# Scan stage of a gated linear recurrence: the sums of squares of seven heads as two f32r products instead of one fp32 product

## The chip, the cores and the metric

One NeuronCore of a Trainium2 chip runs the whole program, a chain of two small transformer blocks in float32 at batch 1 and 256 positions. The metric is the device time of one execution in microseconds; before the change its median is 1361.3 us over three runs (1361.16 to 1363.24).

Engines by their names in the profile: PE is TensorE (PEld its weight loads), DVE VectorE, ACT ScalarE, POOL GpSimd, SP SyncE, which issues the weight DMAs. Each engine runs its instructions in program order; they meet through semaphores alone.

## What is computed

The program runs `first_block` and `second_block`, each of two layers with a mixer and a convolutional feed-forward part. The change lies in the HGRN2 mixer of the second block: a gated linear recurrence, forward and backward, of eight heads, followed by an RMS norm of each head's output over its 128 channels.

```python
def rmsnorm(x, g):
    xf = x.astype(F32)
    y = xf * lax.rsqrt(jnp.mean(xf * xf, axis=-1, keepdims=True) + NORM_EPS)
    return (y * g.astype(F32)).astype(x.dtype)

def mixer_hgrn2(u, mem_kv, w_in, lb_fwd, lb_bwd, norm_g, w_out):
    ...
    o = (gla_chunked(q, k_f, v, lf_f)
         + flip_t(gla_chunked(flip_t(q), flip_t(k_b), flip_t(v), flip_t(lf_b))))
    o = rmsnorm(o, norm_g.reshape(HG_HEADS, HG_VAL_DIM)).reshape(bsz, t, HG_W).astype(u.dtype)
    o = o * jax.nn.silu(gate)
    return jnp.concatenate([o, memory_cross_attn(xq, mem_kv)], axis=-1) @ w_out
```

The mean of squares in `rmsnorm` is what the change touches.

## The kernel before

Every weight matrix is streamed from HBM in tiles of 128 x 2048 floats into three buffers `raw`. ACT copies a tile into `whi` with rounding to f32r (L296), and DVE (L319), POOL (L304) or both subtract this from the original to give the low part `wlo`. Activations are kept in the same way as a high and a low part, in `XS` (input of a mixer) and `MS` (its output, 12 chunks; `ms_high` on ACT, L528, and `ms_low` on DVE, L532). A projection is then the high weights times both parts of the activations (L388, L389), and the low weights times the high part (L395); the output projection is L460 and L471 in the same manner.

The scan stage works on 128 channels of one head on the partitions and 256 positions on the free axis. It is a software pipeline written out by hand, with a loop over n in `hgrn_pe`, `hgrn_act` and `hgrn_dve`; the order of the calls in these loops is each engine's order. In step n, PE projects z of head n, forms the values of head n-2 (`values_pe`, L2306, into the PSUM bank HVAL), projects q and the gate of head n, sums the squares of head n-2 (`squares_pe`, L2315), and forms the scores of head n-1 (`scores_pe`, L2282 to L2295). "Head h" below means the step in which its squares are summed, n = h + 2; from n = 8 on PE works on the output projection in place of z and q.

ACT in step n: logarithms of the gates (L2349, after a table load L2343), a weight copy L296, the exponentials (L2358 to L2360), the root of head n-3 (`root_act`, L2398 and L2400: logarithm, then exponential), a table load and two sigmoids of z (L2369, L2370), a weight copy, the squares of head n-2 (L2379: it reads HVAL and writes SR in SBUF), `ms_high` of head n-3, and the sigmoid of q and gate (L2387).

DVE in step n: gates (L2484, L2485), masks on the scores of head n-2 (L2516, L2517) with four small additions (L2523), the running sums and their differences of head n-1 (L2493 to L2509), a low weight part of 2048 columns (L319), the factors of head n-1 (L2535 to L2549, the last of them L2546), the normed output of head n-3 (L2468), then `UG`, value times gain times gate of head n-2 (L2472), then `ms_low` of head n-3 (L532), and a low part of 1024 columns (L319).

Two orders matter. DVE's L2472 waits for the squares L2379 of the same head (`h_sr`), since two engines don't read a PSUM bank at a time here. ACT's L2358 waits for DVE's differences (`h_di`). POOL takes the other 1024 columns of a low part; in steps 1 and 2 it starts once L2546 is done, in steps 3 to 7 once `ms_low` L532 is done, after the loop once the last L2546 is done.

The sum over partitions is a product with a matrix of ones: `C("ones")` as weights, the squares as moving data, the result on all 128 partitions of HSUM. Both are float32, and PE runs a float32 product as more than one pass.

Of the kernel before, what the change touches and what calls it, by code (L numbers as in the profile page):

```python
# [7 lines left out]
F32 = mybir.dt.float32  # L8
# [3 lines left out]
ALU = mybir.AluOpType  # L12
ACT = mybir.ActivationFunctionType
# [160 lines left out]
def program(nc, T, out):  # L174
    with ExitStack() as ctx:
        pe, ve, ac, po, sp = nc.tensor, nc.vector, nc.scalar, nc.gpsimd, nc.sync

        def sem(name):
            return ctx.enter_context(nc.semaphore("s_" + name))

        def mark(name):
            return Mark(sem(name))

        def sb(name, shape, dt=F32):
            return ctx.enter_context(nc.sbuf_tensor(name, shape, dt))
# [5 lines left out]
        MS = sb("MS", [128, 12, 512], F32R)  # L191
# [22 lines left out]
        def C(name, rows=128):  # L214
            a, b = CC[name]
            return cc[0:rows, a:b]

        def col(name, i=0, rows=128):
            a = PC[name][0] + i
            return pc[0:rows, a:a + 1]  # L220
# [124 lines left out]
        def act_weights(m):  # L345
            while ahead["act"] <= min(m, NTILE - 1):
                high_part(ahead["act"])
                ahead["act"] += 1
# [672 lines left out]
        def soft_act(h, base, s, P, NM, segs, sink=None):  # L1021
            nm, p = NM[h % 4], P[h % len(P)]
            ac.wait_ge(a_mx.sem, base + h + 1)
            if h >= len(P):
                ac.wait_ge(a_tn.sem, base + h - len(P) + 1)
            for i, (a, b) in enumerate(segs):
                ins = ac.activation(p[:, a:b], s[h % 2][:, a:b], ACT.Exp, bias=nm[:, i:i + 1], accum_out=nm[:, 2 + i:3 + i])
            if sink is not None:
                ins = ac.activation(nm[:, 6:8], nm[:, 0:2], ACT.Exp, bias=sink[0])
            ins.then_inc(a_ex.up())  # L1030
# [825 lines left out]
        def cross_query_act(X, j):  # L1856
            ac.wait_ge(w_done, DONE[X.m0 + j])
            ac.activation(X.XQ[:, 512 * j:512 * j + 512], X.pbank[j][:, :], ACT.Copy,
                          scale=float(np.float32(128 ** -0.5))).then_inc(X.xq.up())
# [313 lines left out]
        SR, RS = R(256), R(256)  # L2173
# [11 lines left out]
        MAIN, DIAG, HVAL, HSUM = bank[4], bank[5], bank[6], bank[7]  # L2185
# [6 lines left out]
        h_vn, h_sz, h_sq, h_gt, h_lf = (mark("h_" + k) for k in ("vn", "sz", "sq", "gt", "lf"))  # L2192
        h_di, h_de, h_fa, h_sc, h_mk = (mark("h_" + k) for k in ("di", "de", "fa", "sc", "mk"))

        h_va, h_sr, h_su, h_rs, h_ug, h_on = (mark("h_" + k) for k in ("va", "sr", "su", "rs", "ug", "on"))
        lo0 = PC["lbl"][0]
        l0, l1 = pc[:, lo0:lo0 + 16], pc[:, lo0 + 16:lo0 + 32]
# [2 lines left out]
        def at_z(h):  # L2200
            return ht + 2 * h

        def at_q(h):
            return ht + 2 * h + 1
# [104 lines left out]

        def squares_pe(h):  # L2310

            pe.wait_ge(h_sr.sem, h + 1)
            if h:
                pe.wait_ge(h_rs.sem, h)
            pe.matmul(HSUM[:, 0:256], C("ones")[:, 0:128], SR, start=True, stop=True).then_inc(h_su.up())  # L2315

        def hgrn_act():
            act_weights(hx + 1)
            ac.wait_ge(l_e.sem, 2)
            ac.activation(lb[:, 16:48], lb[:, 16:48], ACT.Exp).then_inc(l_x.up())  # L2320
            act_weights(hw)
            cross_query_act(X1, 0)
            act_weights(hw + 1)
            cross_query_act(X1, 1)
            act_weights(hw + 2)
            soft_act(0, HB, xS, hP, hNM, csegs)
            soft_act(1, HB, xS, hP, hNM, csegs)
            act_weights(at_z(0))
            copy_act(0, HB, xT, hPT, 512)
            soft_act(2, HB, xS, hP, hNM, csegs)  # L2330
            soft_act(3, HB, xS, hP, hNM, csegs)
            act_weights(at_q(0))
            for tt in range(2):
                for h in range(2):
                    ac.wait_ge(w_done, DONE[hw + 2] - 1 + tt)
                    ac.activation(HV[:, tt, 512 * h:512 * h + 512], accs[tt][h][:, :], ACT.Copy).then_inc(h_vn.up())
            act_weights(at_z(1))
            cross_split_act(0)
            cross_split_act(1)
            for n in range(11):  # L2340
                if 0 <= n - 1 < 8:
                    h = n - 1
                    nc.scalar.preload_act_table_set("natural_log_exp_and_others")  # L2343
                    ac.wait_ge(h_sz.sem, h + 1)
                    if h:
                        ac.wait_ge(h_di.sem, h)
                    for d in range(2):
                        o = 8 * d + h
                        ins = ac.activation(lf[:, d, 1:257], SZ[:, 256 * d:256 * d + 256], ACT.Ln, bias=lm[:, o:o + 1],  # L2349
                                            scale=e0[:, o:o + 1])  # L2350
                    ins.then_inc(h_lf.up())
                if n:
                    act_weights(min(at_z(n + 1), LAST[6]))
                if 0 <= n - 1 < 8:
                    ac.wait_ge(h_di.sem, h + 1)
                    if h:
                        ac.wait_ge(h_fa.sem, h)
                    ac.activation(PP, DD, ACT.Exp).then_inc(h_de.up())  # L2358
                    ac.activation(NN, DD, ACT.Exp, scale=-1.0).then_inc(h_de.up())
                    ac.activation(EG, AA, ACT.Exp).then_inc(h_de.up())  # L2360
                if 0 <= n - 3 < 8:
                    root_act(n - 3)
                if n < 8:
                    ac.wait_ge(w_done, DONE[at_z(n)])
                    if n >= 2:
                        ac.wait_ge(h_fa.sem, n - 1)
                    if n:
                        ac.wait_ge(h_lf.sem, n)
                    ac.activation(SZ, BZ[n % 2][:, :], ACT.Sigmoid)  # L2369
                    ac.activation(SN[n % 2], BZ[n % 2][:, :], ACT.Sigmoid, scale=-1.0).then_inc(h_sz.up())  # L2370
                if n == 0:
                    copy_act(2, HB, xT, hPT, 512)
                act_weights(min(at_q(n + 1), LAST[6]))
                if 0 <= n - 2 < 8:
                    h = n - 2
                    ac.wait_ge(h_va.sem, h + 1)
                    if h:
                        ac.wait_ge(h_su.sem, h)
                    ac.activation(SR, HVAL[:, 0:256], ACT.Square).then_inc(h_sr.up())  # L2379
                if 0 <= n - 3 < 8:  # L2380
                    ac.wait_ge(h_on.sem, n - 2)
                    ms_high(n - 3, ON[(n - 3) % 2])
                if n < 8:
                    ac.wait_ge(w_done, DONE[at_q(n)])
                    if n:
                        ac.wait_ge(h_gt.sem, n)
                    ac.activation(SQ, BQ[n % 2][:, :], ACT.Sigmoid).then_inc(h_sq.up())  # L2387
                if n == 0:
                    cross_split_act(2)
                    cross_split_act(3)  # L2390
            act_weights(NEXT[6])
# [14 lines left out]
        def cross_split_dve(i):  # L2406
            ms_low(8 + i, xT[i % 2][:, 0:256])

        def hgrn_dve():
# [41 lines left out]
            dve_weights(at_q(1))  # L2451
            cross_split_dve(2)
            cross_split_dve(3)
            for n in range(1, 11):
                if n - 1 < 8:
                    gates_dve(n - 1)
                if 0 <= n - 2 < 8:
                    masked_dve(n - 2)
                if n - 1 < 8:
                    differences_dve(n - 1)  # L2460
                dve_weights(min(at_z(n + 1), LAST[6]))
                if n - 1 < 8:
                    factors_dve(n - 1)
                if 0 <= n - 3 < 8:
                    h = n - 3
                    ve.wait_ge(h_rs.sem, h + 1)
                    ve.wait_ge(h_ug.sem, h + 1)
                    ve.tensor_tensor(ON[h % 2], UG[h % 2], RS, ALU.mult).then_inc(h_on.up())  # L2468
                if 0 <= n - 2 < 8:
                    h = n - 2  # L2470
                    ve.wait_ge(h_sr.sem, h + 1)
                    ve.scalar_tensor_tensor(UG[h % 2], HVAL[:, 0:256], col("bng", h), GT[h % 2], ALU.mult,  # L2472
                                            ALU.mult).then_inc(h_ug.up())
                if 0 <= n - 3 < 8:
                    ve.wait_ge(h_on.sem, n - 2)
                    ms_low(n - 3, ON[(n - 3) % 2])
                dve_weights(min(at_q(n + 1), LAST[6]))
# [354 lines left out]
```

## Time and profile before

| | |
|---|---|
| median of three runs | 1361.3 us |
| span of the profiled execution | 1361.3 us |
| PE busy | 1337.7 us, 98% |
| DVE busy | 1023.2 us, 75% |
| ACT busy | 783.7 us, 58% |
| POOL busy | 147.7 us, 11% |
| granted clock of PE, mean | 0.998 |
| scan stage | about 1028 to 1167 us |

The page gives busy time of each engine over the whole span. "Waits" give, for a stretch, who waited for whom. A timeline row reads: start and length in us, engine, line and operation, output and inputs by their tiles' names (`ar` is the arena that holds SR, UG and most of the stage's data, `ps` a PSUM bank, `cc` the constants), shapes, how many instructions are merged (xN), and in brackets how long the engine stood idle before it and what ended that. Instructions of one engine overlap a little: the next may start before the one ahead has ended.

### The profile page before, as it was taken

What the parts mean: (1) busy time and instruction counts of PE and PEld (TensorE: products, weight loads), DVE (VectorE), ACT (ScalarE), POOL (GpSimd) and SP (SyncE); (2) the same over time, 40 slices, a digit from 0 to 9 for tenths busy, and PEclk for the clock granted to TensorE, in tenths of its full rate; (3) what the DMA queues carried; (4) which work ended last, traced back from release to release, by engine and by line L of the source; (5) the groups of instructions that cost most, each with busy time, mean ns of one, the idle gap of its engine ahead of it and who ended that gap; (6) DMA issues with size and microseconds to landing.
All of it is one profiled execution on the core that took longest, in us unless ns stands there. A gap on an engine that the chain in (4) does not pass through costs nothing. (4 is left out here: it accounts for less than half of the span.)

```text
span 1361.3 us, 20748 instructions
## 1 busy us (share of the span) xinstructions
PE 1337.7 (98%) x8197; PEld 1160.3 (85%) x8197; DVE 1023.2 (75%) x1681; ACT 783.7 (58%) x1268; POOL 147.7 (11%) x131
## 2 busy tenths in 40 slices
PE   7999999999999999999999999999999999999998
PEld 7887888888898788887987888888789998888887
DVE  5866578777896788778788677666567997786765
ACT  5644266666443566554677566555557875655553
POOL 4770300000100000000000000000302224000000
PEclk9999999999999999999999999999999999999999
DMA  8623165655563455553543255555344345455551
GB/s 315 230 80 125 62 222 213 238 196 198 191 237 138 169 202 218 194 196 136 205 156 112 96 214 216 216 188 189 150 159 182 129 152 186 150 190 204 192 196 73
DMA packets 38175, 242.17 MB, mean 178 GB/s; under 512 B 4416, under 2 KB 6848, under 8 KB 10688
## 3 DMA queue, kind: packets, MB, share of 16 engines
q1 hardware_dynamic: 38080, 240.86, 48.5%
q8 instruction: 65, 1.06, 0.3%
q14 instruction: 30, 0.25, 0.1%
HBM read 236.89 MB, written 2.64 MB: 176 GB/s over the span
## 5 line engine op out<-in xcount | busy, mean ns | idle before, releaser
L319 DVE TENSOR_TENSOR wlo<-raw,whi 128x2048 fp32r<-128x2048 f32 (+1 forms) x179 | 401.2, 2246 | 102.4 <-ACT whi L296 100.4
L296 ACT ACTIVATE whi<-raw 128x2048 fp32r<-128x2048 f32 x195 | 370.5, 1904 | 83.7 <-PE ps L471 39.8
L408 PE MATMUL ps<-XS,whi 128*128 128x512 f32 x1392 | 331.7, 390 | 0.0
L408 PEld LDWEIGHTS ps<-XS,whi 128*128 128x128 f32 x1392 | 257.8, 188 | 52.1 <-issue 0.6
L460 PE MATMUL ps<-whi,MS 128*128 128x512 f32 x960 | 233.5, 391 | 0.0
L460 PEld LDWEIGHTS ps<-whi,MS 128*128 128x128 f32 x960 | 177.5, 188 | 35.9 <-issue 0.4
L413 PEld LDWEIGHTS ps<-XS,wlo 128*128 128x128 f32 x1392 | 178.5, 191 | 6.8
L413 PE MATMUL ps<-XS,wlo 128*128 128x256 f32 x1392 | 180.6, 283 | 0.0
L388 PE MATMUL ps<-XS,whi 128*128 128x256 f32 x672 | 168.0, 290 | 0.0
L389 PE MATMUL ps<-XS,whi 128*128 128x256 f32 x672 | 164.4, 284 | 0.0
L304 POOL TENSOR_TENSOR wlo<-raw,whi 128x512 fp32r<-128x512 f32 x90 | 124.2, 1410 | 195.0 <-ACT whi L296 107.0
L1540 ACT ACTIVATE ar<-ps 128x256 f32<-128x256 f32 x176 | 57.3, 377 | 146.1 <-PE ps L413 145.9
L388 PEld LDWEIGHTS ps<-XS,whi 128*128 128x128 f32 x672 | 129.6, 193 | 1.1 <-issue 0.3
L389 PEld LDWEIGHTS ps<-XS,whi 128*128 128x128 f32 x672 | 129.7, 193 | 0.4
L547 POOL TENSOR_TENSOR st<-st 128x1 f32<-128x1 f32 x24 | 16.7, 696 | 984.9 <-DVE st L724 521.5
L471 PE MATMUL ps<-wlo,MS 128*128 128x512 f32 x480 | 122.5, 389 | 0.0
L471 PEld LDWEIGHTS ps<-wlo,MS 128*128 128x128 f32 x480 | 90.1, 188 | 18.8
L1566 DVE TENSOR_TENSOR ar<-ps,ar 128x256 f32<-128x256 f32 x176 | 66.1, 418 | 43.4 <-ACT ar L1540 43.4
L395 PE MATMUL ps<-XS,wlo 128*128 128x256 f32 x672 | 88.4, 283 | 0.0
L395 PEld LDWEIGHTS ps<-XS,wlo 128*128 128x128 f32 x672 | 84.1, 192 | 0.0
L1546 ACT ACTIVATE ar<-ar,pc 128x256 f32<-128x256 f32 x88 | 40.1, 502 | 46.9 <-DVE ar L1566 46.9
L528 ACT ACTIVATE MS<-ar 128x256 fp32r<-128x256 f32 x104 | 42.2, 405 | 22.6 <-DVE ar L1595 9.6
(330 smaller groups left out, 1546.3 us busy)
## 6 DMA issues: line engine op xcount, KB each, us to landing
raw<-in_up SPq DMA_DIRECT2D x88, 1024.0 KB, 4.8
raw<-in_down SPq DMA_DIRECT2D x44, 1024.0 KB, 4.9
raw<-in_hg_t SPq DMA_DIRECT2D x16, 1024.0 KB, 4.8
raw<-in_od_t SPq DMA_DIRECT2D x8, 1024.0 KB, 5.6
raw<-in_ev_a SPq DMA_DIRECT2D x6, 1024.0 KB, 9.2
raw<-in_wa_o SPq DMA_DIRECT2D x6, 1024.0 KB, 4.9
raw<-in_hg_o SPq DMA_DIRECT2D x6, 1024.0 KB, 4.9
raw<-in_ev_o SPq DMA_DIRECT2D x4, 1024.0 KB, 5.9
```

The costliest lines, as they stand in the source:

```text
L296: ac.activation(parts_of(m)[0][:, 0:w], raw[m % NRAW][:, 0:w], ACT.Copy).then_inc(w_hi)
L304: ins = po.tensor_tensor(lo[:, c], r[:, c], hi[:, c].bitcast(F32), ALU.subtract)
L319: ve.tensor_tensor(lo[:, c], r[:, c], hi[:, c].bitcast(F32), ALU.subtract).then_inc(w_lo_v)
L388: pe.matmul(d, hi[:, c], XS[:, k, 0:256], start=(k == 0 and i == some[0]), stop=False)
L389: pe.matmul(d, hi[:, c], XS[:, k, 256:512], start=False, stop=False)
L395: last = pe.matmul(d, lo[:, c], XS[:, k, 0:256], start=False, stop=(k == 7 and i == some[-1]))
L408: pe.matmul(banks[i][:, 0:512], hi[:, c], XS[:, k, 0:512], start=(k == 0), stop=False)
L413: last = pe.matmul(banks[i][:, 0:256], lo[:, c], XS[:, k, 0:256], start=False, stop=(k == 7))
L460: pe.matmul(accs[tt][h][:, 0:c], x, hi[:, n * j + c * h:n * j + c * h + c], start=(begin and x is sh), stop=False)
L471: ins = pe.matmul(accs[tt][h][:, 0:c], sh, lo[:, n * j + c * h:n * j + c * h + c], start=False, stop=end)
L1540: ac.activation(o[:, 256 * i:256 * i + 256], b[:, 256:512], ACT.Copy).then_inc(f_cb.up())
L1566: ins = ve.tensor_tensor(o[:, c], up_banks(k, j)[i][:, 0:256], o[:, c], ALU.add)
```

## The change

For heads 0 to 6 ACT computes the square twice from HVAL: once rounded to f32r into `SRh` (a part of MS chunk 7, not yet in use), then as before in float32 into `SR`. DVE subtracts, SRl = SR - SRh, right behind L2472. PE multiplies a matrix of ones in f32r (`ONE`, in MS chunk 6, copied once ahead of the loop) with SRh as soon as that is there, and then with SRl, and adds both in HSUM. Head 7 keeps the float32 product, since MS chunk 7 and 6 are needed by then for the mixer's output. New semaphores are `h_sh` (SRh written) and `h_sl` (ONE and SRl written).

```diff
--- before.py
+++ after.py
@@ -2192,6 +2192,8 @@
         h_vn, h_sz, h_sq, h_gt, h_lf = (mark("h_" + k) for k in ("vn", "sz", "sq", "gt", "lf"))
         h_di, h_de, h_fa, h_sc, h_mk = (mark("h_" + k) for k in ("di", "de", "fa", "sc", "mk"))
 
+        h_sh, h_sl = mark("h_sh"), mark("h_sl")
+        ONE, SRh, SRl = MS[:, 6, 0:128], MS[:, 7, 0:256], MS[:, 7, 256:512]
         h_va, h_sr, h_su, h_rs, h_ug, h_on = (mark("h_" + k) for k in ("va", "sr", "su", "rs", "ug", "on"))
         lo0 = PC["lbl"][0]
         l0, l1 = pc[:, lo0:lo0 + 16], pc[:, lo0 + 16:lo0 + 32]
@@ -2309,10 +2311,17 @@
 
         def squares_pe(h):
 
-            pe.wait_ge(h_sr.sem, h + 1)
+            if h == 7:
+                pe.wait_ge(h_sr.sem, h + 1)
+                pe.wait_ge(h_rs.sem, h)
+                pe.matmul(HSUM[:, 0:256], C("ones")[:, 0:128], SR, start=True, stop=True).then_inc(h_su.up())
+                return
+            pe.wait_ge(h_sh.sem, h + 1)
             if h:
                 pe.wait_ge(h_rs.sem, h)
-            pe.matmul(HSUM[:, 0:256], C("ones")[:, 0:128], SR, start=True, stop=True).then_inc(h_su.up())
+            pe.matmul(HSUM[:, 0:256], ONE, SRh, start=True, stop=False)
+            pe.wait_ge(h_sl.sem, h + 2)
+            pe.matmul(HSUM[:, 0:256], ONE, SRl, start=False, stop=True).then_inc(h_su.up())
 
         def hgrn_act():
             act_weights(hx + 1)
@@ -2376,6 +2385,10 @@
                     ac.wait_ge(h_va.sem, h + 1)
                     if h:
                         ac.wait_ge(h_su.sem, h)
+                    if h < 7:
+                        ac.activation(SRh, HVAL[:, 0:256], ACT.Square).then_inc(h_sh.up())
+                    if h:
+                        ac.wait_ge(h_sl.sem, h + 1)
                     ac.activation(SR, HVAL[:, 0:256], ACT.Square).then_inc(h_sr.up())
                 if 0 <= n - 3 < 8:
                     ac.wait_ge(h_on.sem, n - 2)
@@ -2451,6 +2464,7 @@
             dve_weights(at_q(1))
             cross_split_dve(2)
             cross_split_dve(3)
+            ve.tensor_copy(ONE, C("ones")[:, 0:128]).then_inc(h_sl.up())
             for n in range(1, 11):
                 if n - 1 < 8:
                     gates_dve(n - 1)
@@ -2471,6 +2485,9 @@
                     ve.wait_ge(h_sr.sem, h + 1)
                     ve.scalar_tensor_tensor(UG[h % 2], HVAL[:, 0:256], col("bng", h), GT[h % 2], ALU.mult,
                                             ALU.mult).then_inc(h_ug.up())
+                    if h < 7:
+                        ve.wait_ge(h_sh.sem, h + 1)
+                        ve.tensor_tensor(SRl, SR, SRh.bitcast(F32), ALU.subtract).then_inc(h_sl.up())
                 if 0 <= n - 3 < 8:
                     ve.wait_ge(h_on.sem, n - 2)
                     ms_low(n - 3, ON[(n - 3) % 2])
```

## Rows read from the trace of the kernel before

**Rows 1.** Page, busy time of each engine, its share and instructions.
```profile
PE 1337.7 (98%) x8197; PEld 1160.3 (85%) x8197; DVE 1023.2 (75%) x1681; ACT 783.7 (58%) x1268; POOL 147.7 (11%) x131
```

**Rows 2.** Waits, 1040 to 1175 us: who waited for whom, total, times, longest.
```profile
ACT gb L2358 <- DVE ar L2509: 19.5, 7, 4.3
...
DVE ar L2472 <- ACT ar L2379: 5.3, 7, 1.2
...
DVE ar L2516 <- PE ps L2295: 1.7, 4, 0.8
...
PEld ps L2282 <- DVE ar L2546: 0.6, 1, 0.6
...
PEld ps L2315 <- ACT ar L2379: 0.2, 1, 0.2
```

**Rows 3.** Timeline of PE: start, us, instruction (heads 0, 1 and 4).
```profile
1055.17 0.60 PE L2315 MATMUL ps<-ar,cc 128*128 128x256 f32 x2
...
1069.60 0.60 PE L2315 MATMUL ps<-ar,cc 128*128 128x256 f32 x2
...
1070.13 0.28 PE L2282 MATMUL ps<-ar 128*32 128x32 f32 x7
...
1112.95 0.70 PE L2315 MATMUL ps<-ar,cc 128*128 128x256 f32 x2
...
1113.58 0.23 PE L2282 MATMUL ps<-ar 128*32 128x32 f32 x2
```

**Rows 4.** Timeline of PE, two f32r products of a projection.
```profile
1078.76 0.28 PE L388 MATMUL ps<-XS,whi 128*128 128x256 f32 x1
...
1078.88 0.28 PE L389 MATMUL ps<-XS,whi 128*128 128x256 f32 x1
```

**Rows 5.** Timeline of ACT, heads 1 to 5.
```profile
1068.37 0.39 ACT L2379 ACTIVATE ar<-ps 128x256 f32<-128x256 f32 x1
...
1068.63 0.43 ACT L528 ACTIVATE MS<-ar 128x256 fp32r<-128x256 f32 x1
...
1112.51 0.38 ACT L2379 ACTIVATE ar<-ps 128x256 f32<-128x256 f32 x1
...
1127.24 0.38 ACT L2379 ACTIVATE ar<-ps 128x256 f32<-128x256 f32 x1
```

**Rows 6.** Timeline of DVE, head 1.
```profile
1068.79 0.48 DVE L2472 SCALAR_TENSOR_TENSOR ar<-ps,pc,ar 128x256 f32<-128x256 f32 x1 [0.76 <-ACT ar L2379]
...
1069.19 0.41 DVE L532 TENSOR_TENSOR MS<-ar,MS 128x256 fp32r<-128x256 f32 x1
...
1069.52 1.22 DVE L319 TENSOR_TENSOR wlo<-raw,whi 128x1024 fp32r<-128x1024 f32 x1
```

**Rows 7.** Timelines of DVE and POOL, head 0.
```profile
1054.35 0.49 DVE L2472 SCALAR_TENSOR_TENSOR ar<-ps,pc,ar 128x256 f32<-128x256 f32 x1 [0.29 <-ACT ar L2379]
...
1054.75 1.81 DVE L319 TENSOR_TENSOR wlo<-raw,whi 128x1024 fp32r<-128x1024 f32 x1
...
1057.43 0.69 DVE L2516 TENSOR_TENSOR ar<-ps,cc 128x512 f32<-128x512 f32 x1 [0.21 <-PE ps L2295]
...
1054.18 3.52 POOL L304 TENSOR_TENSOR wlo<-raw,whi 128x512 fp32r<-128x512 f32 x2 [9.39 <-DVE ar L2546]
```

**Rows 8.** Timelines of DVE, POOL and PE, head 6.
```profile
1140.97 1.43 DVE L2546 TENSOR_TENSOR ar<-ar 128x256 f32<-128x256 f32 x4
...
1142.65 0.48 DVE L2472 SCALAR_TENSOR_TENSOR ar<-ps,pc,ar 128x256 f32<-128x256 f32 x1
...
1143.29 0.87 DVE L532 TENSOR_TENSOR MS<-ar,MS 128x256 fp32r<-128x256 f32 x1 [0.16 <-ACT MS L528]
...
1142.48 5.33 POOL L304 TENSOR_TENSOR wlo<-raw,whi 128x512 fp32r<-128x512 f32 x4 [8.88 <-DVE ar L2546]
...
1142.45 0.22 PE L2282 MATMUL ps<-ar 128*32 128x32 f32 x1 [0.24 <-DVE ar L2546]
```

**Rows 9.** Timeline of DVE ahead of the loop's first differences.
```profile
1032.70 0.62 DVE L2493 TENSOR_REDUCE ar<-ar 128x14 f32<-128x448 f32 x1 [1.33 <-ACT ar L2349]
```

**Rows 10.** Busy time by window: PE, PEld, DVE, ACT, POOL, granted clock, DMA.
```profile
1170.00:1180.00 10.00, 9.03 (x74) 8.55 (x74) 7.64 (x11) 6.62 (x10) 0.55 (x1) 1.00 0.01 2
```

## The prediction

> **What bounds the kernel now.** I read the page's busy line first: PE is busy in 98% of the span [rows 1], so at first sight every TensorE nanosecond saved is a nanosecond of the result. The waits of the scan stage (1040 to 1175 us) say something more particular [rows 2]. PE hardly waits there: 0.2 us once for the square L2379, 0.6 us once for DVE's factors L2546. But ACT and DVE wait for each other in every step: L2358 waits for DVE's L2509 seven times, 19.5 us in total, and L2472 waits for the square L2379 seven times, 5.3 us. Two engines that wait for each other once a step form a loop, and a loop has a period of its own.
>
> Its period stands in the start times. The squares of head 1 start at 1068.37 us on ACT, those of head 5 at 1127.24: 58.87 us for four heads, 14.72 a head [rows 5]. PE's product of the squares starts at 1055.17 for head 0 and at 1069.60 for head 1: 14.43 a head; by head 4 it starts at 1112.95, (1112.95 - 1069.60) / 3 = 14.45 [rows 3]. So PE is 0.3 us a head faster than the loop and eats a margin. At head 1 the square is there (1068.37 + 0.39 = 1068.76) 0.84 us before PE takes it up at 1069.60. At head 4 the margin is gone: that is the 0.2 us wait. **From head 4 on the DVE and ACT loop sets the pace**, not PE.
>
> The loop, once round: L2472 on DVE, the low part L532, weight splits, gates, masks, differences to L2509; ACT then takes the exponentials from L2358 (which waits 2.8 us a head for L2509, 19.5 / 7), the root, a table load, two sigmoids, a whole weight copy, and the squares L2379; L2472 waits for these. In a step I find no other gap in it that matters.
>
> **The change part by part.** (1) PE. The full fp32 product is two records, 0.60 us together with a mean near 0.38, so the second starts 0.22 us after the first; the first score product starts at 1070.13, 0.53 after 1069.60 [rows 3]. Consecutive f32r products of the same 256 columns start 0.12 apart [rows 4]. Two of them, plus the 0.09 left over before the scores (0.53 less two times 0.22), are 0.33: **0.20 us a head, 1.4 us for seven heads**, where nothing makes PE wait.
>
> (2) ACT gets one more square ahead of the old one. L528 starts 0.26 after L2379 [rows 5], so the old square, and DVE's L2472 behind it, come 0.26 later. L528, the gate sigmoid L2387 and the next table load are queued behind and come as much later, less than what (3) adds on DVE before their results are read. The old square's new wait, for SRl of the head before, ended a round earlier. Lower end nothing, were ACT waiting there anyway (it isn't: L2379 has no idle before it); upper end the whole 0.39 of the square. I take 0.26, the start-to-start time of the nearest pair.
>
> (3) DVE gets the subtraction SRl between L2472 and L532. It has the shape and operands of L532, whose successor L319 starts 0.33 later (1069.19 to 1069.52); L2472's successor starts 0.40 after it [rows 6]. So everything from L532 on comes 0.33 later, GpSimd's split too, which waits for L532. Both pieces lie in the loop: its period goes **from 14.72 to about 15.31**, +0.59 a head.
>
> (4) PE's second product now waits for SRl, and scores and the next z projection are queued behind it. After L2472 starts, SRl ends 0.40 + 0.41 later. A product that was blocked shows the rest of the path: at head 4 the square ended at 1112.51 + 0.38 = 1112.89 [rows 5], the scores started at 1113.58 [rows 3], 0.69 with two slots of 0.22; with one f32r slot of 0.11 it is 0.36. Scores start 1.17 after L2472 starts. For head 1 that is 1068.79 + 0.26 + 1.17 = 1070.22 even with no earlier delay, against 1070.13 now. The saving of (1) is thus behind a wait in every head, and I count it at nothing.
>
> (5) Head 0 is special: GpSimd's split of two operations runs from 1054.18, 3.52 us, and DVE's L319 of 1024 columns, issued at 1054.75, takes 1.81 [rows 7] where it takes 1.22 alone [rows 6]. One of the two engines stands while the other works on SBUF. With L319's 1.1 us inside, a GpSimd operation is (3.52 - 1.1) / 2 = 1.2 to 1.25 us, the first until about 1055.45. After the change L2472 starts at 1054.35 + 0.26, SRl is issued at 1055.01, into that operation; it ends about 1055.78. If GpSimd's second operation then goes ahead of L319 (to 1057.03), L319 ends at 1058.15 instead of 1056.56: 1.59 late, less the 0.3 that the masks L2516 stand now (0.21 idle, and 0.08 of overlap as between L532 and L319): **+1.3**. If L319 goes first it is +0.4 (the scores' end then counts). By the Trainium skill (SBUF — State Buffer, "SBUF: two separate sides") the engine that starts first holds the shared port pair for its whole instruction and the other blocks; the rows agree. GpSimd's second operation is by then the longer waiting, so I take 1.3.
>
> (6) Head 6: scores of head 7 start now when L2546 is done (1140.97 + 1.43 = 1142.40; PE at 1142.45) [rows 8]. DVE runs L2472 only after that, at 1142.65, and now PE must wait for SRl behind it. SRl would be issued at 1143.05, inside GpSimd's operation begun at 1142.48; L532, issued at 1143.29, shows what happens: 0.87 instead of 0.41, end at 1144.15. SRl ends at about that time, scores follow 0.36 later, 1144.51 instead of 1142.45: **+2.05**. Lower end, no contention: SRl ends at 1143.46, +1.37.
>
> (7) The copy of ONE comes before the loop, where DVE is idle 1.33 us before L2493 [rows 9]; some 0.2 us, nothing; were that gap missing it would cost its 0.2 once. No DMA, and nothing on SP's queue, is added or moved. Head 7 is unchanged.
>
> **The sum.** Start of L2472 of head 1: +1.3 (head 0) +0.26. Four more rounds to head 5: 4 x 0.59 = 2.36, so +3.9. There L532 and what follows it come 0.33 later, and so do the factors L2546 of the next step: +4.25. Head 6: +2.05. **PE reaches the scores of head 7 6.3 us late.** From there to the end of the span PE runs one product after another in an order that nothing here shortens, and its waits in the norms are for work that hangs on PE itself; all 6.3 us stay. The profiled execution's span is 1361.3 us, equal to the median of the runs: 1361.3 + 6.3 = **1367.6 us**. With the low ends of (5) and (6): 6.3 - 0.9 - 0.7 = 4.7, 1366.0. With the second square at 0.39 instead of 0.26 in six rounds (+0.8) and the masks' small operations one GpSimd turn later (+0.2): 1368.6.
>
> **The rivals.**
> Rival A, the loop is longer by one of the two pieces only. Some waits that I don't see inside the loop (for GpSimd's split, which stretches the small additions after the masks) could swallow 0.26 or 0.33 a round. For it: DVE also waits 1.7 us in four steps for L2295 of the scores [rows 2], so the loop has soft places. Against: the rounds of heads 1 to 5 average 14.72 though L2516 waits in a part of them only. Five rounds less 0.26 to 0.33 are 1.3 to 1.6 off, 4.7 to 5.0 late; with the low ends of (5) and (6) too, 3.1 to 3.4: 1364.2 to 1366.0, about 1365.3.
> Rival B, the other side: PE stays the bound. If ACT and DVE made up their own lengthening, the second product would find SRl ready and each of seven heads would save 0.20: 1361.3 - 1.4 = 1359.9, that is no measurable change. It decides at the square's end against PE: SRl needs 0.26 + 0.04 + 0.40 + 0.41 + 0.05 = 1.16 us after the old square's end to be ready, less the 0.12 by which the second product comes later. The largest margin in the trace, 0.86 at head 0 (its square ends 0.04 before L2472 starts, at 1054.31; PE is there at 1055.17), is under these 1.04, so it would need a shorter loop than the rows show.
> Rival C, more than the sum: DVE and GpSimd exclude each other at more places than (5) and (6), each turn costing up to 1.25 us: 1368.6 to 1372.
> Rival D, the clock: PE would now stand about 1.1 us in each step. In 1170 to 1180 it stands 0.97 of 10 us and the granted clock is 1.00 [rows 10], the level of 2.4 GHz. By the Trainium skill (Perfetto Trace Analysis, "Matmul Optimizations") the engine scales with utilization, so products should be issued back to back. If the steps of heads 1 to 5, some 75 us, ran at 1.2 GHz the time would be far over 1400 us; the row with as large a share of idle time speaks against it.
> Rival E, that f32r products of this form cost as much as the fp32 one: (1) would be nothing, and the sum hardly moves (+0.1 in head 6), since PE waits for SRl anyway. It is inside the forecast's own range.
>
> **How the numbers follow.** Forecast 0.68 (1366.0 to 1368.6, with E inside), A 0.14, B 0.06, C 0.10, D 0.02. The range takes in the forecast with its bounds, most of A and the nearer part of C: 1364.8 to 1369.8. About 0.2% (2.7 us) is what a measurement of this kernel tells from no change: slower by more means over 1364.0. All of forecast, C, D and nearly all of A: 0.91; within 0.2%: B and a little of A, 0.08; faster by more, 0.01, since (1) gives 0.1% at most.
>
> **What would show it.** In the profile after: L2379's two squares 0.26 apart; starts of L2472 15.3 us apart from head 1 on; PE waiting for DVE's SRl at every head, about 1.1 us a round from head 2 to 5 and about 2 us at head 6; L319 of head 0 stretched well over 1.8 us; L2509 of head 5's step 4.2 us late; nothing given back after the scores of head 7. I am wrong if the starts of L2472 stay 14.7 apart (the loop isn't closed as I say), if PE's waits at the squares are absent (B), or if the lateness at head 7's scores shrinks before the end.

## The result and the profile after

The changed kernel took 1369.88 us in the median of six runs (1368.14 to 1371.92), the kernel before, beside it and earlier, 1361.23 (1360.52 to 1363.24, six runs). The ratio is 1.0062 with a 95% interval of 1.0052 to 1.0072: slower by 8.65 us. On a second chip it was 1370.48 against 1361.75, ratio 1.0065 (1.0052 to 1.0077). Forecast were 1367.6 us and slower; the median lies 2.3 us above the forecast and 0.1 us above the end of the range, 1369.8. Taken by the ratio, 1.0062 times the 1361.3 from which the forecast set out is 1369.7, just inside. The range was met at its very edge, and with nothing to spare.

The profiled execution after has a span of 1366.8 us. Its own time was 1368.14: in every run whose span is on record the time is 1.2 to 1.4 us more than the span, 1.3 in most.

Spans of single executions carry differences that arise long before the stage, so the two profiles are compared from a common mark inside it: the first score product of head 0, before which the change does nothing on PE, to the first score product of head 7, behind which it does nothing either. Timelines of PE, before and then after:

```profile
1041.27 0.28 PE L2282 MATMUL ps<-ar 128*32 128x32 f32 x7
```

```profile
1038.78 0.28 PE L2284 MATMUL ps<-ar 128*32 128x32 f32 x7
```

Before, head 7's scores start at 1142.45 [rows 8]: 101.18 us. After, they start at 1146.38: 107.60. **The stage is 6.42 us longer; the sum said 6.3.** The page in short, after: PE busy 1338.3 us (98%), DVE 1024.0, ACT 784.5, POOL 147.4; the work is hardly more, the order of waits is what changed. The waits of 1040 to 1180 us, against [rows 2] (L2367, L2526, L2486, L2392 are the L2358, L2509, L2472, L2379 of before; L2324 is PE's second product, L2490 DVE's subtraction):

```profile
ACT gb L2367 <- DVE ar L2526: 24.2, 7, 4.8
...
DVE ar L2486 <- ACT ar L2392: 10.0, 7, 4.3
...
PEld ps L2324 <- DVE MS L2490: 7.9, 7, 2.6
```

PE, which hardly waited, now waits for the subtraction in all seven heads, 7.9 us. DVE waits 10.0 us for the square where it waited 5.3. Of these 4.7 us more, the extra square ahead of the one it needs makes 0.27 in each of the heads 0 to 5, 1.6 in all. The other 3.1 are one wait in head 7 (4.25 us, before 1.16), which lies behind head 7's scores and costs nothing, since the time from there to the end is the same as before where the clock doesn't fall (the column "rest" below). Timeline of PE in heads 1 and 6, against [rows 3, 8]; L2322 is the first product, L2324 the second, L2284 the scores:

```profile
1067.53 0.28 PE L2322 MATMUL ps<-MS 128*128 128x256 f32 x1
...
1068.54 0.39 PE L2324 MATMUL ps<-MS 128*128 128x256 f32 x1 [0.74 <-DVE MS L2490]
...
1068.86 0.28 PE L2284 MATMUL ps<-ar 128*32 128x32 f32 x7
...
1146.07 0.39 PE L2324 MATMUL ps<-MS 128*128 128x256 f32 x1 [2.30 <-DVE MS L2490]
...
1146.38 0.28 PE L2284 MATMUL ps<-ar 128*32 128x32 f32 x7
```

The first product starts 1.01 us before the second, ahead of which PE stands idle for the subtraction; the scores follow 0.32 later. At head 6 the stand is 2.30 us long. Timelines of DVE in heads 0, 4 and 5, of ACT in head 4 and of POOL in head 0, against [rows 5 to 7]:

```profile
1052.12 0.48 DVE L2486 SCALAR_TENSOR_TENSOR ar<-ps,pc,ar 128x256 f32<-128x256 f32 x1 [0.56 <-ACT ar L2392]
...
1052.52 0.74 DVE L2490 TENSOR_TENSOR MS<-ar,MS 128x256 fp32r<-128x256 f32 x1
...
1053.18 2.30 DVE L319 TENSOR_TENSOR wlo<-raw,whi 128x1024 fp32r<-128x1024 f32 x1
...
1113.65 0.48 DVE L2486 SCALAR_TENSOR_TENSOR ar<-ps,pc,ar 128x256 f32<-128x256 f32 x1 [1.04 <-ACT ar L2392]
...
1114.05 0.42 DVE L2490 TENSOR_TENSOR MS<-ar,MS 128x256 fp32r<-128x256 f32 x1
...
1114.38 0.42 DVE L532 TENSOR_TENSOR MS<-ar,MS 128x256 fp32r<-128x256 f32 x1
...
1128.97 0.48 DVE L2486 SCALAR_TENSOR_TENSOR ar<-ps,pc,ar 128x256 f32<-128x256 f32 x1 [1.04 <-ACT ar L2392]
...
1112.96 0.38 ACT L2389 ACTIVATE MS<-ps 128x256 fp32r<-128x256 f32 x1
...
1113.22 0.40 ACT L2392 ACTIVATE ar<-ps 128x256 f32<-128x256 f32 x1
...
1051.68 2.71 POOL L304 TENSOR_TENSOR wlo<-raw,whi 128x512 fp32r<-128x512 f32 x2 [9.38 <-DVE ar L2563]
```

In head 4 everything is as in the sum: squares 0.26 apart, L2486 to L2490 0.40, then 0.33, and 15.32 us from one L2486 to the next (1113.65 to 1128.97) where it was 14.72. In head 0 the subtraction L2490 takes 0.74 and L319 of 1024 columns 2.30 instead of 1.81, while GpSimd's two operations take 2.71 together instead of 3.52: they end at 1054.39, and L319 1.09 later, at 1055.48. GpSimd's second operation thus went ahead of L319. Timelines of DVE and POOL in head 6, against [rows 8]:

```profile
1142.85 1.42 DVE L2563 TENSOR_TENSOR ar<-ar 128x256 f32<-128x256 f32 x4
...
1144.92 1.09 DVE L2490 TENSOR_TENSOR MS<-ar,MS 128x256 fp32r<-128x256 f32 x1
...
1145.93 1.50 DVE L532 TENSOR_TENSOR MS<-ar,MS 128x256 fp32r<-128x256 f32 x1
...
1144.35 5.46 POOL L304 TENSOR_TENSOR wlo<-raw,whi 128x512 fp32r<-128x512 f32 x4 [9.11 <-DVE ar L2563]
```

The factors L2563 end at 1144.27; the subtraction, issued at 1144.92, 0.57 after GpSimd began, takes 1.09 instead of 0.41 and ends at 1146.01, and PE starts 0.06 later.

One step is longer than the sum has it: from L2472 of head 5 to the factors. In that step no weight split stands ahead of DVE's masks, and DVE waits there for PE's scores; in the changed kernel these are themselves behind the subtraction. The masks, before and then after:

```profile
1130.04 0.69 DVE L2516 TENSOR_TENSOR ar<-ps,cc 128x512 f32<-128x512 f32 x1 [0.84 <-PE ps L2295]
```

```profile
1131.90 0.69 DVE L2533 TENSOR_TENSOR ar<-ps,cc 128x512 f32<-128x512 f32 x1 [1.11 <-PE ps L2297]
```

They start 2.38 us after L2472 before (at 1127.66), 2.93 after (1128.97): 0.55 later, where the sum has 0.33.

What the sum doesn't hold at all is PE's clock. Busy time by window (PE, PEld, DVE, ACT, POOL, then the granted clock) around the stand at head 6:

```profile
1140.00:1147.00 7.00, 4.70 (x69) 3.63 (x67) 6.90 (x14) 5.55 (x9) 2.65 (x2) 1.00 0.70 263
...
1147.00:1152.00 5.00, 5.00 (x29) 4.13 (x24) 4.06 (x8) 0.63 (x2) 2.81 (x3) 0.66 0.33 93
```

PE was busy 4.70 of 7 us, then the granted clock is 0.66 on average over the next 5 us: part of it at 1.2 GHz in place of 2.4. From head 7's scores to the end of the span it is 220.46 us here and 218.86 before. The kernel before has such a fall as well, but far from the stage, at its start:

```profile
40.00:45.00 5.00, 5.00 (x30) 4.67 (x28) 3.68 (x12) 4.43 (x6) 1.05 (x1) 0.66 1.08 391
```

### The profile page after: what moved, and what is told of

It reads as the page before. It is cut to its first block and busy times, and to the rows that moved or that the text cites. A ratio compares the mean times of both kernels' runs of the same rounds, so it can differ in the third digit from the quotient of the medians.

```text
span 1366.8 us, 20763 instructions
## 1 busy us (share of the span) xinstructions
PE 1338.3 (98%) x8197; PEld 1160.9 (85%) x8197; DVE 1024.0 (75%) x1689; ACT 784.5 (57%) x1275; POOL 147.4 (11%) x131
## 5 line engine op out<-in xcount | busy, mean ns | idle before, releaser
L319 DVE TENSOR_TENSOR wlo<-raw,whi 128x2048 fp32r<-128x2048 f32 (+1 forms) x179 | 401.5, 2248 | 102.2 <-ACT whi L296 100.2
L528 ACT ACTIVATE MS<-ar 128x256 fp32r<-128x256 f32 x104 | 42.1, 405 | 22.3 <-DVE ar L1595 9.6
## 6 DMA issues: line engine op xcount, KB each, us to landing
raw<-in_up SPq DMA_DIRECT2D x88, 1024.0 KB, 4.8
raw<-in_down SPq DMA_DIRECT2D x44, 1024.0 KB, 4.9
raw<-in_hg_t SPq DMA_DIRECT2D x16, 1024.0 KB, 4.8
raw<-in_od_t SPq DMA_DIRECT2D x8, 1024.0 KB, 5.7
raw<-in_ev_a SPq DMA_DIRECT2D x6, 1024.0 KB, 8.9
raw<-in_wa_o SPq DMA_DIRECT2D x6, 1024.0 KB, 4.9
raw<-in_hg_o SPq DMA_DIRECT2D x6, 1024.0 KB, 4.8
raw<-in_ev_o SPq DMA_DIRECT2D x4, 1024.0 KB, 5.9
```

The costliest lines, as they stand in the source:

```text
L319: ve.tensor_tensor(lo[:, c], r[:, c], hi[:, c].bitcast(F32), ALU.subtract).then_inc(w_lo_v)
```

## The experiments

The yardstick in the table is the one above, first scores of head 0 to first scores of head 7 in the profile, less the 101.18 us of before. "Rest" is from there to the end of the span. The last column is the median less that of the kernel before on the same chip, with the interval of the ratio.

| kernel | stage, us | rest, us | median less before, us (ratio, 95%) |
|---|---|---|---|
| before | 0 | 218.86 | |
| changed | +6.42 | 220.46 | +8.65 (1.0052 to 1.0072) |
| changed, again | +6.43 | 220.38 | +8.73 (1.0052 to 1.0077) |
| second square alone | +1.38 | 218.85 | +1.89 (1.0006 to 1.0024) |
| subtraction alone | +2.86 | 218.85 | +2.92 (1.0010 to 1.0027) |
| PE's products alone | -0.18 | 218.85 | -0.12 (0.9987 to 1.0005) |
| changed, head 6 in fp32 | +4.42 | 220.39 | +5.12 (1.0020 to 1.0045) |
| changed, head 0 in fp32 | +5.38 | 220.38 | +6.40 (1.0033 to 1.0060) |
| before, squares early | -0.09 | 220.88 | +0.23 (0.9994 to 1.0012) |
| changed, squares early | +3.23 | 220.73 | +4.85 (1.0024 to 1.0049) |
| both: squares early, head 6 in fp32 | +1.20 | 219.34 | +1.44 (1.0004 to 1.0023) |
| changed, stands filled | +6.46 | 218.87 | +6.28 (1.0033 to 1.0058) |
| before, one stand | +2.37 | 220.48 | +4.93 (1.0019 to 1.0041) |
| before, one stand filled | +2.33 | 218.86 | +3.06 (1.0013 to 1.0031) |

### The three parts, each alone

The second square alone:

```diff
+                    if h < 7:
+                        ac.activation(SRh, HVAL[:, 0:256], ACT.Square).then_inc(h_sh.up())
                     ac.activation(SR, HVAL[:, 0:256], ACT.Square).then_inc(h_sr.up())
```

> The kernel before, with the extra ACT square into SRh alone (nothing reads it; PE keeps its fp32 product, DVE has no subtraction). Loop theory: the period of the DVE and ACT loop grows by 0.26 us to 14.98, six times to the factors that the scores of head 7 wait for: 1.3 to 1.5 us later, 1361.2 + 1.3 = 1362.5 us. PE-bound rival: the square is hidden, 1361.2. Where the clock of PE falls to its lower level now and then because PE stands, about as often as in the kernel before.

The stage came out 1.38 us longer. L2472 (here L2476) on DVE, heads 1 and 5:

```profile
1068.62 0.49 DVE L2476 SCALAR_TENSOR_TENSOR ar<-ps,pc,ar 128x256 f32<-128x256 f32 x1 [1.04 <-ACT ar L2383]
...
1128.60 0.48 DVE L2476 SCALAR_TENSOR_TENSOR ar<-ps,pc,ar 128x256 f32<-128x256 f32 x1 [1.04 <-ACT ar L2383]
```

59.98 us for four rounds, 15.00 each; before, 14.72. The loop takes up 0.28 a round, no less than the start-to-start time of the square, 0.26.

The subtraction alone:

```diff
+                    if h:
+                        ac.wait_ge(h_sl.sem, h)
                     ac.activation(SR, HVAL[:, 0:256], ACT.Square).then_inc(h_sr.up())
 ...
+                    if h < 7:
+                        ve.tensor_tensor(SRl, SR, M32, ALU.subtract).then_inc(h_sl.up())
```

> The kernel before, with DVE's extra subtraction alone (SR minus a tile of constants, 256 columns, SBUF to SBUF, behind L2472; nothing on PE waits for it). Loop theory: +0.33 a round, and in head 0 it meets GpSimd's operation: if GpSimd's second operation then goes ahead of the weight split, +1.3 there, 2.9 us in all, 1364.1 us; if the split goes first, +2.0, 1363.2. PE-bound rival: 1361.2.

It was 2.86 us in the stage and 2.92 in the medians. Heads 1 and 5:

```profile
1069.30 0.48 DVE L2476 SCALAR_TENSOR_TENSOR ar<-ps,pc,ar 128x256 f32<-128x256 f32 x1 [0.76 <-ACT ar L2383]
...
1129.58 0.48 DVE L2476 SCALAR_TENSOR_TENSOR ar<-ps,pc,ar 128x256 f32<-128x256 f32 x1 [0.77 <-ACT ar L2383]
```

15.07 a round, +0.35, and nothing on PE waits for this subtraction: it costs by delaying DVE alone. From the first scores of head 0 to head 1's L2476 it is 28.63 us where it was 27.52: the subtraction of head 0 costs 1.1.

PE's products alone (SRl is a tile of zeros here, so the low part of the squares is left out):

```diff
+            pe.matmul(HSUM[:, 0:256], ONE, SRh, start=True, stop=False)
+            pe.matmul(HSUM[:, 0:256], ONE, SRl, start=False, stop=True).then_inc(h_su.up())
 ...
+                    ac.activation(SRh if h < 7 else SR, HVAL[:, 0:256], ACT.Square).then_inc(h_sr.up())
```

> The kernel before with PE's part alone: heads 0 to 6 as two f32r products, of the f32r square and of a tile of zeros, with no second square and no subtraction, so the low part of the squares is left out. Loop theory: PE saves 0.20 us a head, but from head 4 on it waits for the loop, so only head 0's 0.2 us reaches the end: 1361.0. PE-bound rival: 7 x 0.20 = 1.4 us, 1359.8.

First scores of heads 1, 2 and 7 on PE:

```profile
1055.22 0.28 PE L2284 MATMUL ps<-ar 128*32 128x32 f32 x7
...
1069.44 0.28 PE L2284 MATMUL ps<-ar 128*32 128x32 f32 x7
...
1141.99 0.28 PE L2284 MATMUL ps<-ar 128*32 128x32 f32 x7 [0.61 <-DVE ar L2556]
```

1055.22 to 1069.44 is 14.22 where the round was 14.43: the saving of 0.20 us a head is real while PE leads. But head 7 waits, as before, for the factors (L2546, here L2556), and the stage gains 0.18 in all. Even free of cost on DVE and ACT, PE's part is worth 0.2 us, and the medians can't tell it from nothing.

### The two special heads

Head 6 of the changed kernel in fp32, without second square and subtraction:

```diff
-            if h == 7:
+            if h >= 6:
 ...
-                    if h < 7:
+                    if h < 6:
```

> The changed kernel with head 6 as head 7: fp32 product of SR, no second square, no subtraction, so PE doesn't wait there for DVE's subtraction. Loop theory: the wait of head 6 goes (2.05 us of the sum of 6.3), and the 1.6 us of a fallen clock with it if the long stand of PE at head 6 is what lets it fall: 1361.2 + 4.3 = 1365.5 us. If the clock falls because of the 1.1 us stands in every step instead, the loss above the sum stays: 1361.2 + 8.6 - 2.05 = 1367.8 us.

```profile
1039.53 0.28 PE L2284 MATMUL ps<-ar 128*32 128x32 f32 x7
...
1145.13 0.28 PE L2284 MATMUL ps<-ar 128*32 128x32 f32 x7 [0.25 <-DVE ar L2563]
```

105.60 us between these two, +4.42: **2.00 us** less than the change, where 2.05 were expected. The median is +5.12, between the two expectations for the clock, and the profile has a fall again, this time in the norm behind the stage. So the mechanism of head 6 is shown; what the falls of the clock do is left open by this run.

Head 0 likewise:

```diff
-            if h == 7:
+            if h in (0, 7):
 ...
-                    if h < 7:
+                    if 0 < h < 7:
```

> The changed kernel with head 0 too in fp32 as before (no second square, no subtraction there), heads 1 to 6 as in the change. If DVE's subtraction of head 0 costs more than its own length because it meets GpSimd's operation (GpSimd's second operation goes ahead of the weight split, as the first profile of the change suggests: 1.36 us at the next L2472, 1.1 more than the second square's 0.26), the scores of head 7 start 6.4 - 1.1 = 5.3 us later than before, and the median is that of the changed kernel less 1.1. If head 0 costs no more than any other head (0.59), it is 5.8, 0.6 less.

The stage is +5.38, 1.04 less than the change: head 0 costs 1.04 us where another head costs about 0.6. The next L2472 follows 14.71 us later:

```profile
1053.90 0.48 DVE L2487 SCALAR_TENSOR_TENSOR ar<-ps,pc,ar 128x256 f32<-128x256 f32 x1 [0.29 <-ACT ar L2393]
...
1068.61 0.48 DVE L2487 SCALAR_TENSOR_TENSOR ar<-ps,pc,ar 128x256 f32<-128x256 f32 x1 [1.04 <-ACT ar L2393]
```

15.55 in the changed kernel (1067.67 less 1052.12), and there head 0's own L2486 comes 0.26 later after the first scores of head 0 (13.34 us against 13.08). That makes 1.10 us for head 0, where (5) of the prediction had 1.3.

### Is the loop closed through the squares?

The squares moved ahead of ACT's weight copy, first in the kernel before:

```diff
-                act_weights(min(at_q(n + 1), LAST[6]))
                 if 0 <= n - 2 < 8:
                     ...
+                act_weights(min(at_q(n + 1), LAST[6]))
                 if 0 <= n - 3 < 8:
                     ac.wait_ge(h_on.sem, n - 2)
```

> The kernel before with one move on ACT: the squares L2379 ahead of the weight copy that stood before them, 1.9 us earlier. Loop theory: DVE no longer waits 0.76 us for them, the loop could go round in 13.96 us, under PE's 14.43, so PE sets the pace to head 5: the waits of heads 4 and 5 go (0.05 and 0.3 us) and that of head 6 shrinks, 0.5 to 0.7 us less in all, 1361.5 - 0.6 = 1360.9. Rival (DVE doesn't get ahead, as GpSimd's split and the masks hold it): 1361.5.

My expectation fell: nothing was gained. Timelines of ACT and DVE:

```profile
1109.53 0.39 ACT L2378 ACTIVATE ar<-ps 128x256 f32<-128x256 f32 x1
...
1109.79 1.93 ACT L296 ACTIVATE whi<-raw 128x2048 fp32r<-128x2048 f32 x1
...
1111.60 0.42 ACT L528 ACTIVATE MS<-ar 128x256 fp32r<-128x256 f32 x1
...
1110.90 0.48 DVE L2472 SCALAR_TENSOR_TENSOR ar<-ps,pc,ar 128x256 f32<-128x256 f32 x1
...
1112.12 0.43 DVE L532 TENSOR_TENSOR MS<-ar,MS 128x256 fp32r<-128x256 f32 x1 [0.74 <-ACT MS L528]
```

DVE's L2472 no longer waits for the square, but the next instruction, L532, now waits 0.74 us for ACT's L528, which stands behind the same copy. The loop closes one instruction later and its round is 14.70, as good as the 14.72 of before. PE itself is no longer held at heads 4 and 5 (its scores of head 6 come 0.45 us earlier), but head 7's wait for the factors takes that back. The same with head 6 in fp32 on top of the change:

> The changed kernel with two moves: both squares ahead of the weight copy on ACT, and head 6 in fp32 as head 7. Loop theory: period 15.33 - 1.04 = 14.3, about PE's own 14.2, no wait for DVE's subtraction at head 6; the scores of head 7 wait for the factors L2546 as in the kernel before with the same move: 0.6 us less than the kernel before, 1360.9, where the changed kernel is 6.4 us later. If the order on ACT were not what closes the loop, the time would be that of the change without head 6: 1361.5 + 4.4 = 1365.9.

Also short of what I expected (+1.20 in place of -0.6), for the same reason. Its round is 14.98, and DVE waits for L528 even behind the subtraction:

```profile
1112.88 0.43 DVE L532 TENSOR_TENSOR MS<-ar,MS 128x256 fp32r<-128x256 f32 x1 [0.69 <-ACT MS L528]
```

So the subtraction costs nothing here, as DVE would only have waited longer, and the 0.28 that the round has above 14.70 is the second square alone. It is still 3.2 us less than head 6 in fp32 alone, so the order on ACT carries about half of what the change costs. And the change with the move, head 6 as changed:

> The changed kernel with the squares ahead of ACT's weight copy and head 6 still with its subtraction. With the order alone the loop went round in 14.98 us (with six heads) instead of 15.33, since DVE's L532 then waits for L528 behind the copy. So the scores of head 7 come 1.2 us late as with six heads, plus the wait for the subtraction at head 6, 2.0 us: 3.2 us, against 6.4 for the change, 1361.6 + 3.2 = 1364.8, and up to 1.6 more if the stand at head 6 lets the clock fall. If moving the squares had been worth nothing by itself: 1369.5.

+3.23 in the stage, as expected from the two parts (1.2 and 2.0), and +4.85 in the median; its profile has a fall right at the stand of head 6 (granted clock 0.66 from 1143 to 1148 us). No version with both new pieces beats the kernel before; the best, +1.44 us, is still slower, as its interval lies wholly above 1. The early squares also lengthen the rest by 0.3 to 0.5 us, where L603 of the norm waits 1.5 us for DVE instead of 1.0; I didn't follow that.

### The clock

The changed kernel once more:

> The changed kernel once more, on the same chip as the next three. Loop theory: its scores of head 7 start 6.4 us later after the stage's start than before, as in the first profile; what is above that in the time is falls of PE's clock, about 1.6 us each in the profile. If a fall belongs to the long stand of PE at head 6, its profile has one behind head 6 again, and its median is 1361.5 + 6.4 + 1.6 = 1369.5. If falls come by chance as in every kernel, it is 1361.5 + 6.4 = 1367.9.

The delay in the stage was the same to 0.01 us, the median +8.73. There is a fall in the rest, but not where I expected it: the clock is whole around head 6, where PE stands just as long, and falls in the norm behind the stage.

```profile
1140.00:1152.00 12.00, 9.70 (x98) 7.89 (x96) 11.40 (x23) 7.41 (x12) 3.55 (x3) 1.00 0.69 263
...
1176.00:1186.00 10.00, 8.91 (x61) 8.11 (x58) 7.01 (x13) 4.55 (x10) 1.09 (x2) 0.83 0.01 2
```

The stands filled with work:

```diff
+            for _ in range({0: 0, 6: 16}.get(h, 6)):
+                pe.matmul(HSUM[:, 0:256], ONE, SRh, start=True, stop=True)
             pe.matmul(HSUM[:, 0:256], ONE, SRh, start=True, stop=False)
```

> The changed kernel with the first f32r product of each head repeated where PE stands (6 times more for heads 1 to 5, 0.7 us, and 16 times more for head 6, 1.9 us), each started anew, so the result is the same and PE is busy instead of idle; the order and the waits are the same. Loop theory: the delay stays 6.4 us. If the stands let the clock fall, no fall stands behind head 6 and the median is 1.6 us under that of the changed kernel; if falls come by chance, the same median within the scatter.

```profile
1140.00:1147.00 7.00, 6.59 (x84) 5.59 (x82) 6.90 (x14) 5.54 (x9) 2.67 (x2) 1.00 0.69 266
...
1147.00:1152.00 5.00, 5.00 (x38) 4.22 (x31) 4.21 (x8) 0.61 (x2) 2.83 (x3) 1.00 0.24 91
```

Against the changed kernel PE is busy 6.59 of the same 7 us instead of 4.70, and the clock is 1.00 behind it; it falls nowhere before the last 3 us of the span. The stage is as late as ever (+6.46), but the median is 2.45 us less, and each of its five runs (1366.56 to 1369.18) is below each of the five of the changed kernel on the same chip (1369.43 to 1372.16). This fills the short stands of heads 1 to 5 as well as the long one. Then one stand alone, in the kernel before:

```diff
+            if h == 6:
+                pe.wait_ge(ms_lo.sem, H0 + 10)
             pe.matmul(HSUM[:, 0:256], C("ones")[:, 0:128], SR, start=True, stop=True).then_inc(h_su.up())
```

> The kernel before with one stand of PE alone: the fp32 product of head 6 also waits for the low part L532 behind it on DVE (end at 1144.15 in the first profile instead of a start at 1141.62, 2.5 us). Nothing else is changed. Both theories: the scores of head 7 start 1144.15 + 0.69 = 1144.84 instead of 1142.45, 2.4 us later. If a stand of that length lets the clock fall behind it, the median is 1361.6 + 2.4 + 1.5 = 1365.5, and the profile has a fall within some 40 us behind it; if falls come by chance, 1364.0.

```profile
1139.00:1145.00 6.00, 3.53 (x16) 2.55 (x14) 5.19 (x13) 4.30 (x5) 2.22 (x2) 1.00 0.72 274
...
1145.00:1150.00 5.00, 5.00 (x70) 4.12 (x69) 2.46 (x7) 1.18 (x3) 3.05 (x3) 0.66 0.39 122
```

and the same filled with five more products:

> The same with five more fp32 products of the same squares ahead of the wait (5 x 0.44 = 2.2 us of work in the 2.5 us of the stand); the last product, behind the wait, is started anew, so the result is the same. The delay is the same 2.4 us. If an idle PE is what lets the clock fall, 1361.6 + 2.4 = 1364.0 and no fall behind head 6; if falls come by chance, the same as the kernel with the stand.

```profile
1137.00:1143.00 6.00, 5.77 (x26) 4.46 (x25) 5.25 (x13) 4.30 (x5) 2.17 (x2) 1.00 0.76 270
...
1143.00:1148.00 5.00, 5.00 (x77) 4.11 (x76) 2.96 (x7) 1.19 (x3) 3.13 (x3) 1.00 0.37 124
```

Both are 2.3 to 2.4 us late in the stage. The one that stands idle (3.53 of 6 us busy) has the fall behind it and a rest of 220.48 us; the filled one (5.77 of 6) has neither, 218.86. In the medians they differ by 1.9 us (+4.93, +3.06), though their runs overlap (1361.82 to 1367.28, and 1362.80 to 1366.11), and the intervals of both pairs overlap a little. Where a fall stood in the rest, without early squares, the rest was 1.5 to 1.6 us longer (220.38 to 220.48 against 218.85 to 218.87).

Four profiles have a fall in the norm (changed again, head 0 in fp32, head 6 in fp32, before with squares early). It begins 29.4 to 30.4 us behind the scores of head 7 each time, at the same place in the program, and two of the four have no long stand at head 6. So these falls don't need that stand.

The mean granted clock of every run is on record too, to 0.001. The part that is missing from 1, times the span, is an estimate of the clock that a run lost. On the second chip it is 3.0 us in the mean of 21 runs before, 4.4 in the five changed and 3.0 in the five filled. On the chip of the single stand it is 3.1 before (18 runs), 5.1 with the idle stand (8) and 4.2 with the filled one (11). This goes the way of the two pairs, but a step of the last digit is 1.4 us in one run, so it supports the account and doesn't prove it.

## Why the prediction was right, and where it fell short

**The bound.** Right: the loop of DVE and ACT sets the pace from head 4 on. One reading was off by a head: at head 4 the margin is used up to within 0.06 us, and the wait of 0.2 us for the square belongs to head 5 (PE there at 1127.68). The square alone, off PE altogether, makes every round 0.28 us longer, and PE's saving alone brings 0.18 us in the stage.

**(1), PE's saving of 0.20 a head**: 0.20 in the rounds where PE leads, hidden behind a wait in all seven heads of the changed kernel.

**(2) and (3), +0.26 and +0.33 a round**: 0.28 and 0.35 alone; together the round is 15.32, forecast 15.31. In the last step, from head 5 to the factors, it is 0.56 where the sum has 0.33, because DVE waits there for PE's scores: a path through PE that the prediction left out. With the subtraction alone, for which PE doesn't wait, this step is 0.35 longer (head 5's L2476 to head 6's is 15.34 us, before 14.99), and with the second square alone it isn't longer at all.

**(4), scores 1.17 us after L2472**: 1.19 in head 4 (1113.65 to 1114.84).

**(5), head 0**: with head 1's second square 1.56 were forecast at the next L2472; it came 1.37 later (28.89 us after the first scores of head 0, from 1038.78 to 1067.67; before 27.52, from 1041.27 to 1068.79), and head 0 in fp32 gives 1.04 back where 1.3 were put on it. GpSimd's second operation did go ahead: L319 took 2.30 and ended 1.09 behind GpSimd. By the Trainium skill (SBUF — State Buffer, "SBUF: two separate sides") the engine that starts first holds the shared ports for its whole instruction. These rows agree. Which of two waiting engines is next had to be guessed, and the longer waiting was right here.

**(6), head 6, +2.05**: 2.06 in the profile (the factors end at 1144.27, so without the wait the scores would start 0.05 later as before, at 1144.32, and they start at 1146.38), 2.00 by taking head 6 out.

**(7)** and the statement that nothing is given back behind head 7: right; with ACT's order kept, the rest is the same to 0.02 us wherever the clock doesn't fall between the scores of head 7 and the last 5 us.

**The sum**: 6.3 against 6.42. Its parts were not all exact: head 0 was 0.2 too high and the last step of the loop 0.2 too low. That these two cancel is luck; the rounds and head 6 were right by themselves.

**What failed** is rival D as I had sized it, and with it the last step from the stage to the whole. I asked whether PE's stands would put a long stretch on the lower clock, at far more than 1400 us, and dismissed it with a window of the norm in which PE stands 0.97 us of 10 at full clock [rows 10]. I had already worked out a stand of over 2 us at head 6, twice what that row shows, and never asked what a single short fall costs: 1.6 us in the profile. The medians of the changed kernel are 2.2 and 2.3 us above what the stage lost; filled, its median is within 0.2 us of it. A single fall of 1.6 us doesn't make up all of the 2.2 and 2.3. A second slip lies in the base: I set the span of the profiled execution, 1361.3, equal to the median of the runs, 1361.3. The time of a run is 1.3 us more than its span, so the profiled execution was one of about 1362.6 and held a fall of its own at 41 us. As the forecast set out from that number as a median, it was not moved by the slip.

**The other rivals.** A (only one of the pieces carried) is out by the rounds of 15.32, B (PE stays the bound) by the 7.9 us that PE waits. C (more exclusion between DVE and GpSimd) is not what lies above the forecast: the stage is within 0.12 us of the sum, and the one step that was longer than summed is a wait for PE. E doesn't hold: the f32r products do save 0.20. A's range was also added up wrongly: 3.1 to 5.0 us late is 1364.4 to 1366.3, not 1364.2 to 1366.0; it changes nothing.

**What stays open**: what makes the clock fall, and where it falls in the runs of which there is no timeline. Of five profiles with the long idle stand of head 6, three have the fall right behind it, and two (the changed kernel again, and with head 0 in fp32) have none there but one in the norm, which two kernels without that stand have as well. Of the nine others, the two filled ones among them, none has a fall at head 6. That idle time of PE lets it fall is supported by two pairs that differ in idle time alone, in profile and median, but no kernel except the changed one has a second profile, and of these pairs only the first has runs that don't overlap. That the stand of head 6 accounts for every microsecond above 6.4 isn't shown.

## What to carry to other kernels

An engine busy 98% of the span need not be the one that sets the pace of a stage: compare the start-to-start times of one instruction on each engine over several rounds. Where other engines go round more slowly and the busy one is using up its margin, count every instruction added on them at its start-to-start time per round, unless it falls into a wait that is there anyway, as the subtraction does with the squares early. When a saving on one engine is paid for with work on two others, ask whether those two wait for each other once a round. And when an instruction is made to wait for one placed late in another engine's order, look at the one round in which that order is different (here head 6, whose subtraction comes behind the factors).

## What the runs showed of the hardware that I had not expected

In three of the five profiles in which PE stands idle for 2.3 to 2.8 us at head 6, the granted clock falls within 2 us behind it (0.66 on average over 5 us); in the other two it doesn't. Such a fall makes the rest of the program 1.5 to 1.6 us longer. With a product repeated into the same bank during the stand, the clock stayed at 1.00 there in both profiles in which it was tried.
